# Layer attention: the first probabilities are scaled on ScalarE instead of VectorE, and the reciprocals are taken one unit ahead

## What is computed

```python
def diff_attention(q, k, v, lam):
    def block(args):
        q_blk, qi = args
        s = jnp.einsum('bqhcd,bkhcd->bhcqk', q_blk, k).astype(jnp.float32) * scale
        mask = qi[:, None] >= k_idx[None, :]
        s = jnp.where(mask, s, -jnp.inf)
        pr = jax.nn.softmax(s, axis=-1)
        attn = pr[:, :, 0] - lam * pr[:, :, 1]
        return jnp.einsum('bhqk,bkhe->bqhe', attn.astype(v.dtype), v)
```

## Time and profile before

| what | value |
|---|---|
| time, median of 3 runs (lowest to highest) | 2654.5 us (2652.27 to 2654.7) |
| the profiled execution: its time, its span | 2655.22 us, 2653.4 us |
| busy over the span: PE, DVE, ACT, POOL | 92%, 55%, 30%, 49% |
| layer attention, layer 0: from the first scores matmul to the first output matmul | 172.94 to 222.58 us |
| the same, layer 1 | 841.98 to 891.60 us |
| PE busy within the second of these | 40.32 of 49.7 us |
| mean granted TensorE clock over the span | 0.963 |

### The profile page before, as it was taken

One profiled execution on the slowest core, in us unless ns is written; L12 is line 12 of the kernel. 1 busy time (PEld: TensorE's weight loads), 2 busy tenths in 40 slices (PEclk: granted clock), 3 DMA queues, 4 the chain that ended last, 5 costly groups with the idle time before them and its releaser, 6 DMA issues.

```text
span 2653.4 us, 35939 instructions
## 1 busy us (share of the span) xinstructions
PE 2451.3 (92%) x13296; PEld 2043.3 (77%) x13296; DVE 1451.0 (55%) x1778; ACT 800.4 (30%) x1706; POOL 1303.4 (49%) x1204
## 2 busy tenths in 40 slices
PE   5989999999998999999977799999999997998997
PEld 4657888888765688888855688988988886876776
DVE  7665311233766541121346787787888887226762
ACT  2324210112232420011223324334333332335771
POOL 5733766767774376666752242442444431263003
PEclk9999999999999999999988899999999997899999
DMA  4110344343221033443231011110110111121001
GB/s 151 66 62 32 112 138 142 133 135 104 80 80 64 30 105 128 143 135 127 95 102 64 32 48 47 47 47 32 47 47 32 51 61 57 44 83 48 1 1 48
DMA packets 33543, 199.26 MB, mean 75 GB/s; under 512 B 4384, under 2 KB 6560, under 8 KB 13600
## 3 DMA queue, kind: packets, MB, share of 16 engines
q1 hardware_dynamic: 23040, 162.03, 17.4%
q10 hardware_dynamic: 10400, 35.73, 4.2%
HBM read 192.50 MB, written 5.24 MB: 75 GB/s over the span
## 4 chain that ended last, share of the span: by engine, by line
PE 74%; DVE 16%; issue 5%; ACT 3%; POOL 1%; DMA 0%; ACTq 0%; DVEq 0%; SPq 0%; POOLq 0%
PE ps L381 39%; PE ps L626 11%; PE ps L863 5%; DVE convd L1876 3%; PE ps L744 2%; PE ps L722 1%; PE ps L595 1%; PE ps L761 1%; PE ps L406 1%; PE ps L944 1%; PE ps L961 1%; DVE convd L1890 1%; PE ps L490 1%; PE ps L569 1%; PE ps L731 1%
## 5 line engine op out<-in xcount | busy, mean ns | idle before, releaser
L331 POOL TENSOR_SCALAR whi<-wraw 128x512 fp32r<-128x512 f32 x600 | 409.3, 711 | 1325.7 <-PE ps L626 572.6
L335 POOL TENSOR_TENSOR wlo<-wraw,whi 128x512 fp32r<-128x512 f32 x600 | 899.7, 1531 | 0.0
L381 PE MATMUL ps<-uhi,whi 128*128 128x512 f32 x960 | 382.6, 399 | 37.2 <-DVE ulo L1560 24.8
L381 PE MATMUL ps<-uhi,wlo 128*128 128x512 f32 x960 | 376.0, 392 | 0.0
L381 PE MATMUL ps<-ulo,whi 128*128 128x512 f32 x960 | 375.7, 391 | 0.0
L626 PE MATMUL ps<-inhi,whi 128*128 128x384 f32 (+1 forms) x784 | 249.7, 353 | 30.9 <-ACT raw L1252 17.0
L381 PEld LDWEIGHTS ps<-uhi,whi 128*128 128x128 f32 x960 | 181.6, 189 | 84.2 <-issue 34.6
L626 PE MATMUL ps<-inhi,wlo 128*128 128x384 f32 (+1 forms) x784 | 237.9, 338 | 0.0
L626 PE MATMUL ps<-inlo,whi 128*128 128x384 f32 (+1 forms) x784 | 237.2, 337 | 0.0
L1730 DVE TENSOR_TENSOR h<-h,ps 128x1024 f32<-128x1024 f32 x40 | 48.8, 1221 | 307.5 <-PE ps L381 307.5
L381 PEld LDWEIGHTS ps<-uhi,wlo 128*128 128x128 f32 x960 | 181.4, 189 | 38.5 <-issue 1.9
(11 more groups left out here) (387 smaller groups left out, 4587.2 us busy)
## 6 DMA issues: line engine op xcount, KB each, us to landing
wraw<-in_wstream SPq DMA_DIRECT2D x150, 1024.0 KB, 4.8
modraw<-in_modw ACTq DMA_DIRECT2D x48, 512.0 KB, 3.6
hspill<-hres ACTq DMA_DIRECT2D x1, 3072.0 KB, 8.7
hback<-hspill ACTq DMA_DIRECT2D x1, 3072.0 KB, 9.9
h<-in_x SPq DMA_DIRECT2D x1, 2048.0 KB, 7.3
out<-hfin SPq DMA_DIRECT2D x2, 1024.0 KB, 3.9
gw<-in_gates ACTq DMA_DIRECT2D x2, 512.0 KB, 4.1
pT<-in_pT ACTq DMA_DIRECT2D x2, 512.0 KB, 4.0
```

Of the source, the lines that this page charges most:

```text
L331: pool.tensor_scalar(whi[:, s, c], wraw[:, s, c], 1.0, 0.0, ALU.mult, ALU.add).then_inc(wraw_read, 1)
L335: ins = pool.tensor_tensor(wlo[:, s, c], wraw[:, s, c], whi[:, s, c].bitcast(F32), ALU.subtract)
L381: mm = pe.matmul(ps[:, 2 * bank + m, :], a[:, w, c:c + P], b[:, kb, :], start=(n == 0 and i == 0), stop=(n == KB - 1 and i == 2))
```

## The change

The pass that multiplies the first probability map by its reciprocal goes from DVE to ACT, where it is done in place in `pexp[p, 0]` (`first_scaled`, L1132 of the changed kernel). `combine` keeps one instruction. The reciprocals get a function of their own, which DVE runs for unit n + 1 behind `combine(n)` and `nmax(n + 2)`. Two semaphores are new: `rec_r` (the reciprocals are there; ACT waits for it) and `p1_r` (the scaled map is there; DVE waits for it).

```diff
@@ ACT
+            def first_scaled(n):
+                p, w = n % 2, (n % 4 + 1) * P
+                act.wait_ge(L["rec_r"], l * PER["rec_r"] + n + 1)
+                A(pexp[:, p, 0, 0:w], pexp[:, p, 0, 0:w], ACT.Copy, scale=small[:, 52 + 2 * p:53 + 2 * p]
+                  ).then_inc(L["p1_r"], 1)
+
             exps(0)
+            first_scaled(0)
             for n in range(16):
                 if n + 1 < 16:
                     exps(n + 1)
...
                 A(pattT[:, n % 2, 0:w], ps[:, 6 + n % 2, 0:w], ACT.Copy).then_inc(L["attTc"], 1)
+                if n + 1 < 16:
+                    first_scaled(n + 1)
                 if n % 4 == 0 and n:
                     head_out(n // 4 - 1)
@@ DVE
+            def recips(n):
+
+                p = n % 2
+                dve.wait_ge(L["exp_r"], l * PER["exp_r"] + 2 * n + 2)
+                r1, r2 = 52 + 2 * p, 53 + 2 * p
+                V.reciprocal(small[:, r1:r2 + 1], small[:, 48 + 2 * p:50 + 2 * p]).then_inc(L["rec_r"], 1)
+                dve.wait_ge(L["rec_r"], l * PER["rec_r"] + n + 1)
+                st(V.tensor_tensor(small[:, r2:r2 + 1], small[:, r2:r2 + 1], small[:, 40:41], ALU.mult))
+
             def combine(n):
 
                 p, w = n % 2, (n % 4 + 1) * P
-                dve.wait_ge(L["exp_r"], l * PER["exp_r"] + 2 * n + 2)
-                if n >= 2:
-                    dve.wait_ge(L["att_r"], l * PER["att_r"] + n - 1)
-                r1, r2 = 52 + 2 * p, 53 + 2 * p
-                st(V.reciprocal(small[:, r1:r2 + 1], small[:, 48 + 2 * p:50 + 2 * p]))
-                st(V.tensor_tensor(small[:, r2:r2 + 1], small[:, r2:r2 + 1], small[:, 40:41], ALU.mult))
+                r2 = 53 + 2 * p
+                dve.wait_ge(L["p1_r"], l * PER["p1_r"] + n + 1)
                 if n >= 2:
                     dve.wait_ge(L["attT_r"], l * PER["attT_r"] + n - 1)
-                st(V.tensor_scalar(patt[:, p, 0:w], pexp[:, p, 0, 0:w], small[:, r1:r1 + 1], None, ALU.mult))
                 V.scalar_tensor_tensor(out=patt[:, p, 0:w], in0=pexp[:, p, 1, 0:w], scalar=small[:, r2:r2 + 1],
-                                       in1=patt[:, p, 0:w], op0=ALU.mult, op1=ALU.add).then_inc(L["att_r"], 1)
+                                       in1=pexp[:, p, 0, 0:w], op0=ALU.mult, op1=ALU.add).then_inc(L["att_r"], 1)
 
             nmax(0)
+            nmax(1)
+            recips(0)
             for n in range(16):
+                combine(n)
+                if n + 2 < 16:
+                    nmax(n + 2)
                 if n + 1 < 16:
-                    nmax(n + 1)
-                combine(n)
+                    recips(n + 1)
```

More of the change, by code:

```diff
@@ L251, in build @@
           "attTc", "pv_r", "o_r", "oss_r", "orst_r", "on_r", "ohi_r", "oy_r", "yhi_r", "m_r", "sqh_r", "hlo_r",
-          "pp_ps", "phi_r", "p_r", "pp_r", "g_r", "gth_r", "u_free"]
+          "pp_ps", "phi_r", "p_r", "pp_r", "g_r", "gth_r", "u_free", "rec_r", "p1_r"]
     Ls = {n: sem("L_" + n) for n in LN}
@@ L2305 @@
        "ohi_r": 4, "oy_r": 5, "yhi_r": 1, "m_r": 4 * CHUNKS, "sqh_r": 8 * CHUNKS, "hlo_r": 4 * CHUNKS, "pp_ps": 3,
-       "phi_r": 1, "p_r": 1, "pp_r": 4, "g_r": 4, "gth_r": 4}
+       "phi_r": 1, "p_r": 1, "pp_r": 4, "g_r": 4, "gth_r": 4, "rec_r": 16, "p1_r": 16}
 def softplus(V, st, out, e, z, z2, p):
```

## The result

The changed kernel takes 2659.17 us (median of 10 runs, 2657.56 to 2661.54), the kernel before 2653.01 us beside it (10 runs, 2647.50 to 2656.61). The ratio is 1.0022, with a 95% interval of 1.0014 to 1.0031: slower by 6.2 us, where 5.5 us were forecast. The profiled execution of the changed kernel took 2658.49 us, with a span of 2656.5.

A forecast was written before the change was run, and what follows sets the result against it. A loop of hand-overs between PE, ACT and DVE in the layer attention was taken as the bound. 2 layers x 3 heads x 0.92 = 5.5 us more gave 2660.0 us, 8-in-10 range 2654.5 to 2667.

The forecast's parts named there:

- the thirteen steps: One head of the new attention loop, between width 4 transposes: 10.19 us against 9.27, 0.92 us more.
- steps 3 to 6: Reciprocal and hand-over 0.19 us; ACT's width 2 scaled copy 0.41; head_out 0.97; two exponentials of unit 10 1.24.
- step 8: ACT's scaled copy of unit 10 (width 3), 0.61 us, and a hand-over of 0.04: 0.65 us.
- step 12: ACT's scaled copy of unit 11 (width 4), 0.715 us, and a hand-over of 0.04: 0.76 us.
- let that product leave the path: DVE's product with minus lambda leaves the path, counted at nothing, because the combine waits longer for the scaled copy anyway.
- The branch beside steps 9 to 11: Exponentials and reciprocal of unit 11, beside combine, transposes and their copy: done about 0.1 us earlier, adding nothing.
- the first at nothing: First head of a layer costs nothing: PE at 1.2 GHz and long scores cover the copies; uncovered, up to 0.9 us.
- Nothing for the reciprocals: DVE's reciprocals "one step ahead" bring nothing: they are 0.15 us and still wait for nmax(n + 2).
- C: Rival: ACT has room (8.7 of 9.28 us a head), the copies stay hidden; 2654.5 to 2656 us; chance 0.20.
- D: Rival: faster, as DVE's scaling leaves the chain and nothing replaces it; 1.3 us a head, 2646.6 us; chance 0.08.
- Order.* This is the part that decides: On ACT the scaled copy of unit n + 1 stands behind unit n's transposed-map copy, so must wait for its transposes.
- B: Rival: PE's clock falls more often in the heads; 9 us on top (2669), or 2664.5 in half; chance 0.22.

The follow-up runs named there:

- the kernel with the reciprocal really moved: Changed kernel with DVE's reciprocals of unit n + 1 ahead of the maxima nmax(n + 2) instead of behind them; 2664.71 us (one run).
- the filled kernels: Before and the changed kernel, each with seven matmuls a layer whose result nobody reads; 2649.06 us and 2653.70 us.
- one width only: Changed kernel with the scaled copy on ACT for width 1 alone or width 4 alone, the others on DVE; 2656.76 and 2657.80 us (one run each).
- the folded product: Kernel before with the small product with minus lambda (L1707) folded into DVE's scaling pass; 2650.99 us, ratio 0.9995.
- the filled before: Kernel before with seven matmuls a layer whose result nobody reads, in PE's waits; 2649.06 us, ratio 0.9981.

## Why the prediction was right, step by step

**The loop.** The sum of the thirteen steps was 10.19 us and the head is 10.28. Laid against the timeline from 195.37: step 1 2.22; step 2 1.08; steps 3 to 6 0.19, 0.41, 0.96, 1.24; step 7 0.22; step 8 0.71 (0.65 forecast); step 9 0.67; step 10 0.59; step 11 0.38; step 12 0.80 (0.76); step 13 0.81. The term that was mis-sized is the hand-over from ACT's scaled copy to DVE's combining pass: 0.10 and 0.09 us (202.30 to 202.40 and 204.75 to 204.84) where 0.04 had been taken from the hand-over of DVE to PE. The hand-over enters twice, and these 0.1 us are the whole difference. The chain shows 0.03 of it as an instruction of DVE's queue, the wait of L1723. That wait is also for the transposes, which were over long before, but it isn't they that make the hand-over long. Units 0 and 1 have no wait for transposes, and their hand-over is longer still (unit 0: the scaled copy ends at 175.94 + 0.40, the pass starts at 176.45, 0.11 later). In the kernel with the reciprocal really moved the wait for the transposes is there and the hand-over is 0.03:

```profile
196.41 0.71 ACT L1132 ACTIVATE pexp<-pexp,small 128x512 f32<-128x512 f32 x1
...
197.15 0.75 DVE L1724 SCALAR_TENSOR_TENSOR patt<-pexp,small 128x512 f32<-128x512 f32 x1 [0.32 <-ACT pexp L1132]
```

There the maxima stand between the product with minus lambda (L1715) and the pass, and take the wait for that product. In unit 15 of that kernel no maxima stand between, and the hand-over is 0.09 again (217.84 + 0.72 to 218.65). In the changed kernel the pass always has the wait for the product (`L_d_step`) beside the one for the scaled map. So what goes with the long hand-over is the wait for L1715. The prediction let that product leave the path: its 0.16 us do, but its wait, it seems, does not.

**The prices.** 0.715, 0.61 and 0.51 were forecast, 713, 615 and 508 ns measured. L1043, the row of the same form elsewhere in the kernel, was the right row; L1137, which reads PSUM with a constant scale, was not, although it is the nearer one in the program. The kernel with a constant scale splits the 116 ns between them at 512 columns: 25 between the two plain copies, one from PSUM and one from SBUF (597 against 622), and 91 for the scale from a column.

**The branch beside steps 9 to 11** was said to be done 0.1 earlier. Its reciprocal is (203.85 against ACT free at 204.04), its exponentials tie with the transposes within 0.01. It adds nothing, as forecast, but there is no slack left.

**How many heads.** Three a layer, and the first at nothing: measured 0.95, 1.01, 1.10 and 1.01, 1.01, 1.12, which is 6.20, with 0.03 and 0.14 for the first heads and 0.18 behind the last transposes. 6.55 in all against 5.5. The cover of the first head is shown by the filled kernels. The narrower third head of before (9.18, no further scores behind it) lost the most, which the sum with 9.27 for all three had missed.

**Nothing for the reciprocals** was right for a simpler reason than the one given: they never moved.

**The rivals.** C (room on ACT) falls: ACT is busy 8.66 of 10.28 us, as it had computed (8.7), and the head grew all the same. D falls, and with it the reason given against it. The step of the prediction that failed is "*Order.* This is the part that decides", although the number came out: with the order turned round the head is 10.56, longer than 10.28. So the place behind the copy is not what costs. What costs is the scaled copy on ACT, since with the scaling back on DVE the time is that of before. The kernels with a constant scale and with one width only point to the reason: the copy is one more serial piece between exponentials and combination. B did not happen here: the steady heads run at full clock and the time at 1.2 GHz is the same 17.1 us. Its mechanism is real, though, and was seen in the kernels with a constant scale, with one width only, with the folded product and in the filled before, at up to 1.6 us for a head that it struck (10.6 against 9.04 with the folded product).

**What stays open.** PE's waits in a head were 2.44 us in the changed kernel and the clock held; they were 1.4 in the filled before and it fell. So the sum of the waits in a head does not decide. Where they fall in time may, but no run here isolates that, and which head is struck was not foreseen.

## What to carry to other kernels

When two engines pass one tile back and forth, count the serial pieces between their hand-overs; an engine at 75% busy (6.92 of 9.28 us here) may have no room if its copy stands between its own exponentials and the partner's next pass. Price a new instruction from a row of the same form (where it reads, and where its scale comes from), not from its neighbour, and take the hand-over for that pair of engines and for all that the receiving instruction waits for. Undo each half of a change alone before crediting either: one half of this one was only another way to write the same order.

## What the runs showed of the hardware

- A hand-over from ACT to DVE costs more when the DVE instruction waits for another DVE instruction too. The combining pass starts 0.09 to 0.10 us after ACT's scaled copy where it also waits for L1715, and 0.03 after it where it doesn't (197.12 to 197.15 in the kernel with the reciprocal really moved); the reciprocal, which waits for one semaphore, starts 0.02 to 0.03 after the exponentials (203.65 to 203.68). No run changed this wait alone.
- ACT's copy costs 91 ns more with a scale from a column than with a constant one (713 against 622 ns at 512 columns); DVE's pass costs 60 ns more with two such factors than with one (546 against 486 ns).
- Slow stretches of PE's clock can take back gains of this size. In the filled before, PE's work in 199.00 to 200.00 was 0.24 us and in each of the three microseconds behind it the clock was 0.50, 1.2 GHz:

```profile
199.00:200.00 1.00, 0.24 (x2) 0.24 (x3) 0.96 (x4) 0.81 (x4) 0.00 (x0) 0.99 0.00 0
200.00:201.00 1.00, 1.00 (x7) 1.00 (x5) 0.89 (x5) 0.47 (x2) 0.00 (x0) 0.50 0.00 0
```

The earlier trace rows have a stretch with the same 0.24 us of work (201 to 202) in the kernel before, and the clock stayed full there. For this the Trainium skill has a rule ("TensorE: Matmul & The Clock Gate", section "A second HAM failure mode: psum-queue depth-cycling": frequent short gaps can make the clock swing); the falls in the filled before agree, and the steady heads of the changed kernel, with longer waits and no fall, show that the gaps alone don't say when.
